# GpSimd makes the low parts of all sixteen query chunks, the last two of them between its first gathers

## The reference

```python
def peer(h, w_query, sub_keys, down, up):
    B, S, D = h.shape
    T = B * S
    hf = h.reshape(T, D)
    q = (hf @ w_query).reshape(T, PEER_HEADS, 2, PEER_HALF)      # 1024 x 2048 weights
    s = jnp.einsum('thpd,pkd->thpk', q, sub_keys).astype(jnp.float32)
    sv, si = lax.top_k(s, PEER_TOPK)
    cand = ...      # 256 sums of pairs per token and head
    top_s, top_pos = lax.top_k(cand, PEER_TOPK)
    idx = jnp.take_along_axis(cand_idx, top_pos, axis=-1)
    g = jax.nn.softmax(top_s, axis=-1)
    # per token: pre = h . down[idx];  w = g * gelu(pre);  out = sum w * up[idx]
```

## Time and profile before

| | |
|---|---|
| median of 3 runs | 1850.58 us (1848.67 to 1851.85) |
| profiled execution, its own time | 1846.17 us |
| its span | 1844.4 us |
| TensorE busy | 1583.7 us (86%) |
| VectorE busy | 1319.0 us (72%) |
| GpSimd busy | 621.1 us (34%) |
| ScalarE busy | 547.0 us (30%) |
| chain that ended last | PE 34%, DVE 25%, DMA 25% |

### The profile page before, as it was taken

The page is one execution under the profiler, slowest core; times in us unless marked ns, Lnnn a source line. Parts: engine busy times, 40 slices in busy tenths (PEclk is TensorE's granted clock), DMA queues, the critical chain, the costliest instruction groups (busy, mean ns, idle before and its releaser), DMA issues.

```text
span 1844.4 us, 20738 instructions
## 1 busy us (share of the span) xinstructions
PE 1583.7 (86%) x7052; PEld 1170.7 (63%) x7052; DVE 1319.0 (72%) x2595; ACT 547.0 (30%) x1337; POOL 621.1 (34%) x527
## 2 busy tenths in 40 slices
PE   3998999988997979999999999999999989998000
PEld 2787877766876979888888888884444434443000
DVE  5766456667556598899875888886566566667998
ACT  2433234444623633111116888880000000000001
POOL 1000000000002512534454455456444464445772
PEclk8999999999998989999999999999999999999555
DMA  8423311123421536999998889889999999999995
GB/s 315 159 100 151 137 69 47 70 91 144 187 92 52 188 119 241 350 334 326 373 342 289 319 312 317 320 320 379 409 409 409 411 410 409 409 409 409 377 380 218
DMA packets 124232, 498.19 MB, mean 270 GB/s; under 512 B 13920, under 2 KB 14176, under 8 KB 113760
## 3 DMA queue, kind: packets, MB, share of 16 engines
q0 software_dynamic: 73728, 268.47, 38.5%
q1 hardware_dynamic: 50400, 228.41, 32.9%
HBM read 492.11 MB, written 4.72 MB: 269 GB/s over the span
## 4 chain that ended last, share of the span: by engine, by line
PE 34%; DVE 25%; DMA 25%; ACT 5%; issue 4%; POOL 3%; DVEq 3%; ACTq 1%; SPq 0%; POOLq 0%
DMA ring<-in_up,idx 16%; PE bank L756 9%; DVE accum L1678 8%; DMA ring<-in_down,idx 8%; PE bank L491 6%; PE bank L492 6%; PE bank L493 6%; DVE ring L1460 4%; POOL ring L1703 3%; PE bank L743 2%; DVE acc_ada L1118 2%; DMA raw<-in_ada 1%; ACT h2T L1037 1%; ACT h2T L1042 1%; ACT whi L791 1%
## 5 line engine op out<-in xcount | busy, mean ns | idle before, releaser
L756 PE MATMUL bank<-h2T,stream 128*128 128x256 f32 x2048 | 452.7, 380 | 2.3 <-ACTq L1071 2.3
L769 PE MATMUL bank<-stream,wmat 128*128 128x512 f32 x1024 | 443.5, 596 | 12.1 <-DMA stream<-in_up 8.2
L1703 POOL DMA_INDIRECT ring<-in_down,idx x256 | 306.0, 1195 | 374.5 <-DVE pre L1460 295.9
L1678 DVE SCALAR_TENSOR_TENSOR accum<-ring,share,accum 128x1024 f32<-128x1024 f32 x256 | 328.8, 1284 | 138.3 <-DMA ring<-in_up,idx 129.5
L756 PEld LDWEIGHTS bank<-h2T,stream 128*128 128x128 f32 x2048 | 386.8, 191 | 52.7 <-issue 2.7
L1460 DVE CUSTOM_DVE_ANT_0 ring<-ring,h2row 128x1024 f32<-128x1024 f32 x256 | 307.6, 1220 | 76.5 <-DMA ring<-in_down,idx 74.4
L769 PEld LDWEIGHTS bank<-stream,wmat 128*128 128x128 f32 x1024 | 196.0, 192 | 258.9 <-issue 245.8
L1703 POOL DMA_INDIRECT ring<-in_up,idx x256 | 263.8, 1031 | 211.8 <-DVE accum L1678 172.2
L491 PE MATMUL bank<-hT_hi,whi 128*128 128x512 f32 (+1 forms) x640 | 236.7, 370 | 29.5 <-DVE hT_lo L1171 12.3
L1712 POOL TENSOR_TENSOR wlo<-raw,whi 128x2048 fp32r<-128x2048 f32 x11 | 51.1, 4645 | 608.0 <-ACT whi L791 608.0
L492 PE MATMUL bank<-hT_lo,whi 128*128 128x512 f32 (+1 forms) x640 | 226.2, 353 | 0.0
(11 more groups left out here) (211 smaller groups left out, 1633.7 us busy)
## 6 DMA issues: line engine op xcount, KB each, us to landing
stream<-in_downT SPq DMA_DIRECT2D x128, 512.0 KB, 5.8
stream<-in_up SPq DMA_DIRECT2D x128, 512.0 KB, 6.8
raw<-in_ada SPq DMA_DIRECT2D x24, 1024.0 KB, 5.3
raw<-in_w_query SPq DMA_DIRECT2D x16, 1024.0 KB, 4.8
raw<-in_w_xp SPq DMA_DIRECT2D x4, 1024.0 KB, 6.7
raw<-in_w_gateA SPq DMA_DIRECT2D x4, 1024.0 KB, 4.8
raw<-in_w_branchP SPq DMA_DIRECT2D x4, 1024.0 KB, 4.8
raw<-in_w_q SPq DMA_DIRECT2D x4, 1024.0 KB, 4.8
```

Of the source, the lines that this page charges most:

```text
L756: last = pe.matmul(bank[:, 4 + i % 2, 0:DT], stream[:, i % RING, k * P:(k + 1) * P], h2T[:, k, GB * P:S], start=(k == 0), stop=(k == KT - 1))
L769: last = pe.matmul(bank[:, 2 * tb + half, :], wmat[:, i, tb * P:(tb + 1) * P], stream[:, (ET + i) % RING, half * S:(half + 1) * S], start= ...
L1678: dve.scalar_tensor_tensor(accum[:, b, :], ring[slot][:, :], share[:, b, k:k + 1], accum[:, b, :], ALU.mult, ALU.add).then_inc(sum_done, 1)
L1703: pool.indirect_dma_start(out=ring[slot][:, :], out_offset=None, in_=table, in_offset=bass.IndirectOffsetOnAxis(ap=idx[:, b, k:k + 1], axi ...
```

## The change

GpSimd makes the low parts of all 16 query chunks. It makes those of Q0 to Q13 ahead of its gathers. After gather 1 it makes that of Q14, after gather 3 that of Q15. VectorE makes none of them and stage2(0) runs without anything between. GpSimd's wait for the stored x1 moves from ahead of the gathers' loop into it, behind the wait for the indices.

```diff
-ROUTE_PER_WLO = 4.5
-POOLED = 10
+POOLED = 16
+POOL_FIRST = 14
+POOL_MORE = 2
...
-            split = [QUERY + POOLED, 0.0]
-
-            def fill_lows(us):
-
-                split[1] += us
-                if split[1] >= ROUTE_PER_WLO and split[0] < len(CHUNKS):
-                    follow(split[0])
-                    split[0] += 1
-                    split[1] = 0.0
...
-            stage2(0, fill_lows)
-            while split[0] < len(CHUNKS):
-                follow(split[0])
-                split[0] += 1
+            stage2(0, nothing)
...
-            for n in POOL_CHUNKS:
+            def wlo_make(n):
+
                 if n:
                     pool.wait_ge(lo_ready, n)
                 pool.wait_ge(hi_ready, n + 1)
...
-            pool.wait_ge(x1_stored, 16)
+            for n in POOL_CHUNKS:
+                if n < QUERY + POOL_FIRST:
+                    wlo_make(n)
             for g in range(GB * P):
                 b, k = g // P, g % P
                 if k == 0:
                     pool.wait_ge(idx_ready, b + 1)
+                if g == 0:
+                    pool.wait_ge(x1_stored, 16)
...
                 gather(down, b, k, down_slot[g])
+                late = QUERY + POOL_FIRST + (g + 1) // POOL_MORE - 1
+                if (g + 1) % POOL_MORE == 0 and late < len(CHUNKS):
+                    wlo_make(late)
```

## The result

The changed kernel takes 1854.55 us (median of 16 runs, 1852.1 to 1857.46), the kernel before 1850.71 in the same series (16 runs, 1842.56 to 1855.34). The ratio is 1.0024, 95% interval 1.0013 to 1.0035: slower by 3.8 us (2.4 to 6.5). The profiled execution took 1853.29 us with a span of 1851.1, against 1846.17 and 1844.4; for it the prediction had 1853.8.

A forecast was written before the change was run, and what follows sets the result against it. Bound by a fixed-length transfer tail that starts when TensorE ends its 128 tiles: +10.0 for their later start, -2.35 for a vanished stall, +7.6 us in sum, median 1858.2 us; range for 8 in 10 1851.5 to 1862.5.

The forecast's parts named there:

- GpSimd makes Q10 in time; the loop steps 6.7 and 7.5 by turns: TensorE's query chunks: Q10 starts at 667.1, 8.6 earlier, then steps of 6.7 and 7.5 instead of 6.64.
- VectorE is held twice, 8.8 us, by the low parts of Q11 and Q13: VectorE's stage2: two-input operations wait for GpSimd, losing 8.8 of 14.6 us freed; indices done at 703.6.
- The added wait; Q15 +9.7 to +10.3: Low parts Q14 and Q15 wait behind indices and gathers; TensorE's 128 tiles start 10.0 us later.
- The lower case: Gathers unhindered by VectorE's dots: low part Q15 ends at 719.5, in time, and TensorE starts Q15 at 720.4.
- The slow clock behind the longer stall: TensorE's Q14 after a 17 us stall: slow clock taken as before, 8.48 us for the chunk.
- -2.35 at tile 68: TensorE's stall of 2.35 us, waiting through ScalarE for VectorE's routing, goes because TensorE arrives 10.0 later.
- rival A: VectorE is not held in stage2: indices at 694.9, Q15 +1.1, sum -1.2, time 1849.4 us; chance 11%.
- The median 4.4 above the profiled execution, after as before: Step from the profiled execution's forecast, 1853.8, to the median, 1858.2: 4.4 us added, as in the kernel before.
- Nothing in the tail: The last stretches, with full transfer engines at share 1.02, have fixed length and take back none of the +7.6 us.
- B: Only one of the two holds on VectorE happens: indices at 699.2, Q15 +5.3, sum +3.0, 1853.6 us; chance 11%.
- C: Changing between low parts and gathers costs GpSimd 0.9 more, three times: +2.7, 1860.9 us; or longer slow clock; chance 14%.
- D: The delay does not reach the end, the tail taking it back: 1850.6 us; chance 6%.

The follow-up runs named there:

- experiment 5: The changed kernel, but GpSimd makes no low part for Q11 to Q13 and only signals: 1843.33 us against 1849.43 for the kernel before, ratio 0.9966.
- experiments 9 and 10: The kernel before, without any edit, traced twice more: 1847.19 and 1850.65 us.
- experiments 1 to 8 and 11: Nine runs with edits to the kernel before (1, 6, 7, 11) or to the changed kernel (2 to 5, 8): from 1838.6 to 1854.62 us.
- experiments 1, 5 and 6: Besides experiment 5, two edits of the kernel before: exponentials two tiles later, ratio 0.9983; GpSimd also making the low parts of Q10 and Q12, ratio 0.9982.

## Why the prediction was right, and where it was off

The way to the delay of TensorE came nearly as forecast. The time came 3.7 us under the forecast: 3.1 of this is the step from the profiled execution to the median, 0.5 the sum itself.

- **GpSimd makes Q10 in time; the loop steps 6.7 and 7.5 by turns.** Right: low parts at 661.62, 668.31, 675.78, 682.47.
- **VectorE is held twice, 8.8 us, by the low parts of Q11 and Q13.** Right in size and place (4.44 and 4.41 more than alone); experiment 5 takes it away and the indices move from 703.55 to 695.0. Wrong in the operation: I read from the earlier trace rows that two inputs are what is held, and took the CASTs as free. They are held as well, by either kind. That the sum came out alike was luck: the CASTs stand next to the ones I named.
- **The added wait; Q15 +9.7 to +10.3.** The size is right, +10.0, the way to it in part. I had two gathers held by dots, and low part Q15 late with them at the upper end. One was (1.85, near the 1.91 of the earlier trace rows), the other took 0.95, and low part Q15 was over 0.47 before Q15 started. The lower case, TensorE's own Q14, set the start, and came later than its 720.4 (720.7 with the offset) by the next term.
- **The slow clock behind the longer stall.** Taken as 8.48 for Q14, measured 9.12 (719.96 less 710.84): 0.6 more behind a stall of 16.72 than behind one of 9.16.
- **-2.35 at tile 68.** This is the term that was mis-sized. The row itself, 15.74 us for four tiles that need 13.8, showed 1.93 of slow clock behind the stall; I had priced that behind Q10 and Q14 and not here. With it the two traces agree: 10.0 - 4.3 = 5.7, measured 5.8 at the last matmul. Experiment 5 shows the same: rival A's +1.1 at Q15 came nearly true (tiles +0.8 with the offset), and with 4.3 in the place of 2.35 the last matmul is 3.6 earlier (with the offset).
- **The median 4.4 above the profiled execution, after as before.** A silent step that failed, and the larger part of the miss: the changed kernel's median is 1.3 above its profiled execution and not 4.4. What makes the rest of before's 4.4 is open; a longer loss at tile 68 is the likely part (experiments 9 and 10).
- **Nothing in the tail.** Right to within 2.3 us: 601.0 to 603.3 in thirteen traces (before three times, after, and the nine of experiments 1 to 8 and 11). But 1.7 of this lies between the two compared traces. The profiled execution came out near its forecast (+7.1 for +7.6) in part by luck: the 1.9 too little at tile 68 and the 0.76 of the start are made up by the 1.7 of the tail and 0.4 outside the span.
- **The rivals.** A (not held) is refuted by the trace and by experiment 5. B did not happen, both held, though the time is near B's number. C happened in small and did not count: a gather behind a low part waited 1.02 and 1.01 where 0.30 lies between gathers, a low part behind a gather waited nothing, and Q15 was set by TensorE. D is refuted by experiments 1, 5 and 6.

## What to carry to other kernels

Before work is moved to GpSimd beside a busy VectorE, look in the trace for one row where the two lie together, for each kind of operation: the price is not that GpSimd works for 4.6 us, but that VectorE may stand as long. Put such work under operations that nothing holds, and behind no wait that depends on the engine it holds. And where a profile shows a short stall that another engine sets, price what follows it too, and trace it more than once: its length may be what makes the runs spread.

## What the runs showed of the hardware

- VectorE's CAST (uint32 to bf16 and to float32) stands until the end of a low part that began before it, 4.80 and 4.63. The CAST to bf16 and a TENSOR_SCALAR stand until the end of a write of 16 KB per partition, 3.59 and 3.25. TENSOR_TENSOR with two SBUF inputs stands beside a low part, which reads, and not beside the write (4.55 and 5.46, against 0.29 and 1.23). Searches and match-replace are not held by a low part (FIND_INDEX8 0.23, MATCH_REPLACE8 0.22 beside that of Q12 in the changed kernel); no reduction began beside one. The Trainium skill's page "SBUF — State Buffer", section "Who interferes with whom", says that cast and tensor_scalar can enter modes that contend with GpSimd, and that two SBUF inputs contend with a GpSimd instruction that reads and not with one that only writes; the runs agree.
- A gather is a GpSimd operation too, and does not hold them: in experiment 5 one runs from 723.07 to 724.01, and a CAST that starts at 723.52 beside it takes 0.21. It is the gather that takes longer beside a dot, 1.85 for 0.94.
- A short stall of TensorE may or may not be followed by the slow clock: 2.35 us of idle was followed by a mean granted clock of 0.61 and 15.74 us for four tiles, 3.09 by 1.00 and 14.05, 6.77 by 0.63 and 15.59.
